# A two-block model kernel on Trainium2: feed-forward output by seven half-size products that stay in PSUM

## The chip, the cores and the metric

One core of a Trainium2 chip. The metric is the device time of one launch in microseconds (us); lower is better.

## The reference

All data is fp32, 1024 tokens of width 1024. The model is an attention-and-state-space block, then a feed-forward, then a second block of three gated branches, each with norms and residuals. The change is in the feed-forward of the first block:

```python
h = rmsnorm(x, norm_mlp_pre[l])                                   # 1024 x 1024
f = jnp.square(jax.nn.relu(h @ w_ff_in[l])) @ w_ff_out[l]         # hidden 1024 x 4096, out 1024 x 1024
x = x + rmsnorm(f, norm_mlp_post[l])
# then the second block: h = rmsnorm(x, norm_g_2); p = h @ w_in_2; ...
```

## The kernel before

**Arithmetic.** Every fp32 operand of a matmul is held as a high part (ScalarE copies it into the fp32r type) and a low part (VectorE subtracts the high part from the original). A product is three matmuls: high x high, high x low, low x high. Each takes a 128x128 stationary tile and 512 moving columns, and gives one PSUM bank. The eight banks are `A0a A0b A1a A1b X0a X0b X1a X1b`.

**Order.** There is no scheduler. Each engine runs its own program in the order in which the code is written, and semaphores tie them together. All loads go through one queue, SP's, in the order of its program; a load that waits holds up every load behind it. `FILLS` lists which product fills which bank, in TensorE's order.

**The feed-forward.** The hidden layer has 32 tiles `T` of 128 features by 1024 tokens. Four (`fi` 0 to 3) come first, then 24 from twelve panels `P` (the hidden product by seven half-size products: 7 products of 12 matmuls for a panel of two tiles), then `fi` 28 to 31. Each tile is made in one of three buffers `stage`, squared there by VectorE (`hidden_square`), and stored to HBM (`h_store`, 512 KB). VectorE's part of a panel is in `seven_run`; `seven_sums` makes the sums of weights (S1 to S4) and `seven_lo` the low parts of the weights (WL).

**The output product** (`out_part`) walks the depth of 4096 in eight chunks `c` of 512. For each chunk and each half `n` of the output columns it takes the eight token tiles `m`: 4 depth tiles x 3 matmuls into one bank. So there are 8 x 2 x 8 x 12 = 1536 matmuls. VectorE adds each bank into `F` in SBUF (`f_add`, line 1810). Chunk 0 uses the four tiles made last, which never leave SBUF; those of the other chunks are read back (`h_load`), and `W2H`/`W2L` hold two weight panels of `w_ff_out` split by `hi` (line 897) and `lo` (line 1434).

**The end of it.** For each token tile `m`: `f_square` (ScalarE, line 927), GpSimd's reciprocal root `fo` (lines 2836, 2675, 2676), `f_scale` (VectorE, lines 1886 and 1888: scale, add the residual), `x2_square` (ScalarE; it also stores the tile), GpSimd's root `x2`, `x2_norm` (VectorE, line 1892), `t2_turn` (TensorE transposes the tile, line 2214), and `t2_high`/`t2_low` split it into `XBH`/`XBL`. From these the second block's first products `au` begin. In the last chunk this chain runs tile by tile beside the remaining products.

Of the kernel before, what the change touches and what calls it, by code (L numbers as in the profile page):

```python
# [6 lines left out]
P = 128  # L7
SEQ, D = 1024, 1024
KD = D // P
# [5 lines left out]
TAU = 8  # L15
# [61 lines left out]
single("w2", 2 * FCH)  # L77
# [12 lines left out]
WHOLE = ("wo", "w2", "v2w", "w3", "plw", "P")  # L90
# [58 lines left out]
BANKS4 = ("X0a", "X0b", "X1a", "X1b")  # L149
for _c in range(FCH - 1):  # L150
    FILLS += [(("fo", _c, n, m), BANKS4[m % 4]) for n in range(2) for m in range(MT)]
for _m in range(MT):
    FILLS += [(("fo", FCH - 1, n, _m), BANKS4[(2 * _m + n) % 4]) for n in range(2)]
    if _m >= 3 and _m < 7:
        FILLS.append((("t2", _m - 3), "A%d" % ((_m - 3) % 2)))
FILLS += [(("t2", m), "A%d" % (m % 2)) for m in range(4, 8)]
# [24 lines left out]
for _m in range(MT):  # L181
    RSTD_ORDER += [("fo", _m)] + ([("x2", _m - 1)] if _m else [])
RSTD_ORDER += [("x2", MT - 1)] + [("v2", m) for m in range(MT)]
# [21 lines left out]
def hybrid_kernel(nc, io, out):  # L205
# [4 lines left out]
    with ctx:  # L210
# [83 lines left out]
        F = at("F", [P, MT, D], 34.5)  # L294
        W2H, W2L = at("W2H", [P, 2, KW, W4], 66.5, f32r), at("W2L", [P, 2, KW, W4], 82.5, f32r)
        H = at("H", [P, 5, 2, SEQ], 164.5, f32r)
        HS = at("HS", [P, 5, 2, SEQ], 164.5)
        HB, HBS = at("HB", [P, 8, 2, SEQ], 100.5, f32r), at("HBS", [P, 8, 2, SEQ], 100.5)
        post2, pre3 = at("post2", [P, D], 180.5), at("pre3", [P, D], 184.5)
        xr2 = [at("xr2_%d" % m, [P, D], (116.5 + 4 * m if m < 4 else 148.5 if m == 4 else 34.5 + 4 * (m - 5)))  # L300
# [64 lines left out]
        h_scr = dram("h_scr", [FF, SEQ])  # L365
# [35 lines left out]
        hs_ready, hidden_hi, hidden_lo = sem("hidden_squared"), sem("hidden_hi"), sem("hidden_lo")  # L401
# [65 lines left out]
        def stage_of(p, h):  # L467

            return 4 + 2 * p + h

        def hidden_of(raw_form, u):

            c, i = u // 4, u % 4
            if c in (0, 2, 4, 7):
                return (HS if raw_form else H)[:, (3, 4, 1, 0)[i]]
            return (HBS if raw_form else HB)[:, i + (4 if c == 6 else 0)]


        h_in = u_in

        def hidden_in(eng, c):
            eng.wait_ge(h_in[c % 2], 16 + 64 * ((c + 1) // 2))
# [9 lines left out]
        def _(sp):  # L492
# [10 lines left out]
            def panel(key, src):  # L503
                s = panel_free(key)
                dst = rawk[:, s] if key[0] == "w2" else raw[:, s, 0:DEPTH_K.get(key[0], KD), :]
                sp.dma_start(dst, src).then_inc(w_in_s[s], 16)
# [161 lines left out]
            wf2 = io["w_ff_out"].rearrange("o (k p) n -> p (o k) n", p=P)  # L668
# [4 lines left out]
            def w2_panel(c, n):  # L673
                g = (c - 1) % FCH
                panel(("w2", 2 * c + n), wf2[:, KW * g:KW * (g + 1), W4 * n:W4 * (n + 1)])
# [14 lines left out]

            def h_store(T):
                sp.wait_ge(hs_ready, T + 1)
                sp.dma_start(h_scr[T * P:(T + 1) * P, :], stage[T % 3][:]).then_inc(x1_out[T % 3], 16)

            def h_load(c):
                if c in (2, 3, 4, 5, 7):
                    filled(sp, ("fo", c - 3 if c == 7 else c - 2, 1, MT - 1))
                for u in range(4 * c, 4 * c + 4):
                    T = u - 4
                    staged(sp, T % 3, T // 3 + 1)  # L700
                    sp.dma_start(hidden_of(True, u)[:, 1, :], h_scr[T * P:(T + 1) * P, :]).then_inc(h_in[c % 2], 16)
            for p in RUNS[0][0]:
                seven_panel(p, wf1, 2 * P * (p + 2))
                h_store(2 * p)
                h_store(2 * p + 1)
            fi_panel(LAST_HIDDEN)
# [18 lines left out]
            for m in range(5):  # L725
                x1_in(m)
# [2164 lines left out]
```

## Time and profile before

| | |
|---|---|
| median of 3 runs | 2157.14 us (2157.02 to 2157.6) |
| the profiled execution | 2156.99 us, of which the span in the trace is 2155.3 us |
| granted TensorE clock, mean | 0.996 of full |
| TensorE busy | 2110.9 us, 9828 matmuls |
| VectorE, ScalarE, GpSimd busy | 1151.8, 749.1, 266.0 us |
| HBM traffic | 178.71 MB read, 62.39 MB written, 112 GB/s over the span |

The times of single matmuls in the trace overlap (they are pipelined and their ends are modelled), so a stage of TensorE is measured from start to start. Times of a row are counted from the start of the span.

### The profile page before, as it was taken

To read this page: it belongs to the slowest core of one execution; us is meant where nothing else is said; L and a number is where in the kernel's file an instruction comes from. 1 tells how busy PE (TensorE), PEld (TensorE's weight loads), DVE (VectorE), ACT (ScalarE), POOL (GpSimd) and SP (SyncE) were. 2 spreads that over 40 slices of the span, in tenths; PEclk is the share of its full clock that TensorE was granted. 3 is DMA by queue.
4 is the path that set the end of the run, shared out by engine and by line. 5 is a ranking of instruction groups with operands and counts; after the bars stand their busy time and mean duration, and the time that the engine had idled before them with its cause. 6 is when DMAs were issued, how large, how long until landed. Compare 5 with 4: busy or idle time off the path is not lost.

```text
span 2155.3 us, 24566 instructions
## 1 busy us (share of the span) xinstructions
PE 2110.9 (98%) x9828; PEld 1746.7 (81%) x9828; DVE 1151.8 (53%) x1326; ACT 749.1 (35%) x1112; POOL 266.0 (12%) x507
## 2 busy tenths in 40 slices
PE   7999999989999999999999999999999999999998
PEld 6888888877888888878888878888888888878877
DVE  4226666837458566423444467666444666535552
ACT  4236666143324444333111234224444333222121
POOL 1376295000110000000000021200000000000100
PEclk9999999999999999999999999999999999999999
DMA  5543323676312333322234153113323221424332
GB/s 152 120 99 103 118 93 101 168 241 231 131 69 88 108 118 118 118 98 79 78 119 155 40 185 113 40 49 108 118 106 110 79 78 64 147 97 147 117 118 108
DMA packets 169989, 243.88 MB, mean 113 GB/s; under 512 B 26995, under 2 KB 128020, under 8 KB 169620
## 3 DMA queue, kind: packets, MB, share of 16 engines
q1 hardware_dynamic: 160400, 219.64, 30.7%
q10 hardware_dynamic: 9476, 22.67, 3.3%
q8 instruction: 78, 1.28, 0.2%
q14 instruction: 35, 0.29, 0.0%
HBM read 178.71 MB, written 62.39 MB: 112 GB/s over the span
## 4 chain that ended last, share of the span: by engine, by line
PE 83%; DVE 7%; issue 4%; ACT 2%; DMA 1%; SPq 1%; POOL 1%; DVEq 0%; POOLq 0%; ACTq 0%
PE A L2160 7%; PE A L2162 7%; PE A L2161 7%; PE X L2422 6%; PE X L2423 6%; PE X L2424 6%; PE X L2497 5%; PE X L2496 5%; PE X L2498 5%; PE A L2497 4%; PE A L2496 4%; PE A L2498 4%; PE X L2160 2%; PE A L2422 2%; PE A L2423 2%
## 5 line engine op out<-in xcount | busy, mean ns | idle before, releaser
L1427 DVE TENSOR_TENSOR WL<-raw,WH 128x1024 fp32r<-128x1024 f32 (+1 forms) x110 | 115.2, 1048 | 270.9 <-ACT WH L891 270.8
L891 ACT ACTIVATE WH<-raw 128x1024 fp32r<-128x1024 f32 (+1 forms) x110 | 97.3, 885 | 302.8 <-PE A L2162 159.6
L2160 PE MATMUL A<-XH,WH 128*128 128x512 f32 x384 | 151.9, 396 | 0.0
L2162 PE MATMUL A<-XH,WL 128*128 128x512 f32 x384 | 149.8, 390 | 0.0
L2161 PE MATMUL A<-XL,WH 128*128 128x512 f32 x384 | 149.7, 390 | 0.0
L1441 DVE TENSOR_TENSOR WL<-S,WH 128x512 fp32r<-128x512 f32 x128 | 88.1, 689 | 104.3 <-ACT WH L916 103.2
L1810 DVE TENSOR_TENSOR F<-F,X 128x512 f32<-128x512 f32 x112 | 75.5, 685 | 126.9 <-PE X L2424 126.8
L1441 DVE TENSOR_TENSOR WL<-raw,WH 128x512 fp32r<-128x512 f32 x96 | 66.1, 688 | 108.4 <-ACT WH L916 108.3
L916 ACT ACTIVATE WH<-S 128x512 fp32r<-128x512 f32 x128 | 80.4, 628 | 116.9 <-PE X L2498 62.1
L2496 PE MATMUL X<-TH,WH 128*128 128x512 f32 x280 | 109.1, 390 | 0.0
L2498 PE MATMUL X<-TH,WL 128*128 128x512 f32 x280 | 109.1, 389 | 0.0
L2497 PE MATMUL X<-TL,WH 128*128 128x512 f32 x280 | 109.0, 389 | 0.0
L2422 PE MATMUL X<-W2H,H 128*128 128x512 f32 x256 | 101.1, 395 | 5.1 <-DVE H L1857 2.7
L897 ACT ACTIVATE W2H<-rawk 128x2048 fp32r<-128x2048 f32 x16 | 30.6, 1914 | 214.9 <-PE X L2424 214.9
L2423 PE MATMUL X<-W2L,H 128*128 128x512 f32 x256 | 100.3, 392 | 0.0
L2424 PE MATMUL X<-W2H,H 128*128 128x512 f32 x256 | 100.3, 392 | 0.0
L2423 PE MATMUL X<-W2L,HB 128*128 128x512 f32 x256 | 99.7, 390 | 0.0
L2424 PE MATMUL X<-W2H,HB 128*128 128x512 f32 x256 | 99.7, 390 | 0.0
L2422 PE MATMUL X<-W2H,HB 128*128 128x512 f32 x256 | 99.7, 389 | 0.0
L2496 PE MATMUL A<-TH,WH 128*128 128x512 f32 x232 | 90.4, 390 | 1.0 <-DVE WL L1441 1.0
L2160 PE MATMUL A<-XBH,WH 128*128 128x512 f32 x232 | 90.8, 391 | 0.0
L2162 PE MATMUL A<-XBH,WL 128*128 128x512 f32 x232 | 90.4, 390 | 0.0
(550 smaller groups left out, 5399.1 us busy)
## 6 DMA issues: line engine op xcount, KB each, us to landing
raw<-in_w_in SPq DMA_DIRECT2D x49, 1024.0 KB, 5.5
raw<-in_w_ff_in SPq DMA_DIRECT2D x16, 1024.0 KB, 5.4
rawk<-in_w_ff_out SPq DMA_DIRECT2D x16, 1024.0 KB, 9.3
h_scr<-stage SPq DMA_DIRECT2D x28, 512.0 KB, 2.6
g_scr<-stage SPq DMA_DIRECT2D x24, 512.0 KB, 3.6
g_scr<-gst ACTq DMA_DIRECT2D x32, 256.0 KB, 2.8
x_scr<-xr ACTq DMA_DIRECT2D x16, 512.0 KB, 2.8
HBS<-h_scr SPq DMA_DIRECT2D x16, 512.0 KB, 6.1
```

Source lines behind the costliest of these rows:

```text
L891: A(unit_home(WH[:, r % 2, 0:kb, :], key), unit_of(raw[:, SLOT[p], 0:kb, :], key, i), ACT.Copy).then_inc(w_hi, 1)
L1427: TT(unit_home(WL[:, r, 0:kb, :], key), unit_of(raw[:, SLOT[p], 0:kb, :], key, i), unit_home(WH[:, r, 0:kb, :], key).bitcast(f32), ALU.sub ...
L1441: TT(seven_home(WL, p, j), seven_weights(p, j), seven_home(WH, p, j).bitcast(f32), ALU.subtract).then_inc(w_lo, 1)
L2160: mm(dst, WH[:, r, k, :], xh, start=(k == 0), stop=False)
L2161: mm(dst, WH[:, r, k, :], xl, start=False, stop=False)
L2162: return mm(dst, WL[:, r, k, :], xh, start=False, stop=(k == kb - 1))
L2422: mm(dst, xh, wh(k), start=(k == 0), stop=False)
L2423: mm(dst, xh, wl(k), start=False, stop=False)
L2424: last = mm(dst, xl, wh(k), start=False, stop=(k == kb - 1))
L2496: mm(psum(key), high[:, i, :], xh, start=opens and i == 0, stop=False, skip_group_check=not opens)
L2497: mm(psum(key), high[:, i, :], xl, start=False, stop=False, skip_group_check=not opens)
L2498: last = mm(psum(key), low[:, i, :], xh, start=False, stop=i == KW - 1, skip_group_check=not opens)
```

## The change

The output product is now made from seven half-size products. Tokens, output columns and the depth are each cut in two: tokens into 0 to 511 and 512 to 1023, output columns into 0 to 511 and 512 to 1023, and the depth into its even and its odd tiles of 128 (a "pair" q is the tiles 2q and 2q+1). Each of the seven products j has 512 tokens x 2048 of depth x 512 columns: four token tiles, four chunks c of four depth tiles, three matmuls each. `STEPS` lists their 28 steps (j, c), each of 48 matmuls, in the order: products 0 and 1 by turns over their four chunks, then 2 and 3 by turns, then 4, 5, 6. Each product keeps its four banks over its whole depth; products 2 and 4 go on accumulating on product 1's banks, 3 and 5 on product 0's (`OUT_OPENS` names those that start from nothing). So a bank is read once in four steps, by `product_copies` (ScalarE), `join` or `last_join` (VectorE), and `f_add` is gone.

- **Hidden side.** While the hidden tiles are made, VectorE makes four sums and differences of halves of each pair (`hidden_sum`, 4 x 128x512 for each of 16 pairs) in `SB`. SP stores 256 KB of the even tile, 512 KB of the odd one, and 1 MB of sums of each pair to `a_scr`, seven half-width forms in all, in place of 512 KB a tile. The last four tiles go through memory too. A `stage` buffer is reused only when its sums are made (`summed_past`).
- **Weight side.** Products 1 to 4 need a sum of quarters of `w_ff_out`, which VectorE makes in place from what was loaded (`weights_sum`, 128x2048, one a step). Those of product 3 are stored to `w_scr` and read again for product 4.
- **Loads.** 64 loads of 1 MB for the steps go through a ring of eight 8 KB buffers (four from product 5 on; the first four loads have homes of their own). Each waits until the last user of its buffer is split. A pair of steps of products 0 and 1 takes 4 loads, of 2 and 3 takes 5 and a store, a step of 4 takes 3, of 5 and 6 takes 2.
- **Splits.** Each step splits its weights and its hidden data into `W2H`/`W2L` and `H2H`/`H2L` (two buffers each), one step ahead: `split_high` waits until the step before last is done.
- **Norms.** The chain of tiles 0 to 3 now runs beside steps 20 to 25 (r = s - 21 in the code of VectorE), the one of tiles 4 to 7 after `last_join`. Their residual rows lie in the buffers of the weight panels, so panels `au` 2 and `v2w` 0 are loaded when these tiles have been stored.

```diff
+STEPS = [(j, c) for js in ((0, 1), (2, 3), (4,), (5,), (6,)) for c in range(CHUNKS) for j in js]
...
-            for c in range(FCH - 1):
-                for n in range(2):
-                    for m in range(MT):
-                        out_part(c, n, m)
...
+            for s in range(STEP[6, 2]):
+                r = s - STEP[5, 0]
+                if r in (2, 3, 4, 5):
+                    out_step(s, range(2))
+                    t2_turn(r - 2)
+                    out_step(s, range(2, 4))
+                else:
+                    out_step(s)
+            out_step(STEP[6, 2], range(3))
+            out_step(STEP[6, 3], range(1))
+            out_step(STEP[6, 2], range(3, 4))
+            out_step(STEP[6, 3], range(1, 4))
+            t2_turn(4)
+            first_half(("au", 0), xb, "t2", 0)
             t2_turn(5)
...
+            def out_step(s, ms=range(4)):
+                j, c = STEPS[s]
+                if ms[0] == 0:
+                    pe.wait_ge(out_lo, 2 * s + 2)
+                opens = j in OUT_OPENS
+                for m in ms:
+                    key = ("S", j, m)
+                    if c == 0:
...
+                        begin(key)
+                    for k in range(KW):
+                        high, low = H2H[:, s % 2, k, P * m:P * (m + 1)], H2L[:, s % 2, k, P * m:P * (m + 1)]
+                        mm(psum(key), high, W2H[:, s % 2, k, :], start=opens and c == 0 and k == 0, stop=False, ...)
+                        mm(psum(key), high, W2L[:, s % 2, k, :], start=False, stop=False, ...)
+                        last = mm(psum(key), low, W2H[:, s % 2, k, :], start=False, ...)
...
+            def split_high(s):                                   # ScalarE
+                if s >= 2:
+                    step_past(act, s - 2)
...
+                A(W2H[:, s % 2], out_weights(s), ACT.Copy).then_inc(out_hi, 1)
+                landed(act, (j, c, "hidden"))
+                A(H2H[:, s % 2], out_hidden(s), ACT.Copy).then_inc(out_hi, 1)
...
+            def split_low(s):                                    # VectorE
+                dve.wait_ge(out_hi, 2 * s + 1)
+                TT(W2L[:, s % 2], out_weights(s), W2H[:, s % 2].bitcast(f32), ALU.subtract).then_inc(out_lo, 1)
+                dve.wait_ge(out_hi, 2 * s + 2)
+                TT(H2L[:, s % 2], out_hidden(s), H2H[:, s % 2].bitcast(f32), ALU.subtract).then_inc(out_lo, 1)
...
+            for s in range(2, len(STEPS)):                       # VectorE
+                r = s - STEP[5, 0] - 1
+                if 1 <= r < 5:
+                    x2_norm(r - 1)
+                split_low(s)
+                if s + 1 < len(STEPS) and STEPS[s + 1][0] in SUMMED:
+                    weights_sum(s + 1)
...
+                if r == 3:
+                    join(5, 0, part(4, 1), part(4, 1))
+                    join(5, 1, part(5, 1), part(5, 1))
+                if 0 <= r < 4:
+                    f_scale(r)
...
-                if m:
+                if m % 4:                                        # GpSimd: order of the roots
                     x2_rstd(m - 1)
-            x2_rstd(7)
+                if m % 4 == 3:
+                    x2_rstd(m)
```

**First place: VectorE at the start of the twelve panels.** TL are low parts of token sums, S and WL as above, `stage` rows are squares. Before:

```order
L1820 TENSOR_TENSOR TL1_195<-TR1_191,TH1_187 128x2048 [waits t_hi,t_sum]
L1455 TENSOR_TENSOR S1_202<-raw_49 128x512 [waits w_loaded1]
L1455 TENSOR_TENSOR S2_203<-S1_202,raw_49 128x512 [waits s_sum]
L1441 TENSOR_TENSOR WL_52<-raw_49,WH_51 128x512 [waits w_hi]
L1441 TENSOR_TENSOR WL_52<-S1_202,WH_51 128x512 [waits w_hi]
L1820 TENSOR_TENSOR TL2_196<-TR2_192,TH2_188 128x2048 [waits t_hi]
L1769 TENSOR_TENSOR stage2_211<-stage2_211 128x1024 [waits evicted_A0]
L1455 TENSOR_TENSOR S3_204<-raw_49 128x512
L1455 TENSOR_TENSOR S4_205<-raw_49,S2_203 128x512 [waits s_sum]
L1820 TENSOR_TENSOR TL3_197<-TR3_193,TH3_189 128x2048 [waits t_hi]
L1441 TENSOR_TENSOR WL_52<-S2_203,WH_51 128x512 [waits w_hi]
```

The same place of the change:

```order
L1992 TENSOR_TENSOR TL1_205<-TR1_201,TH1_197 128x2048 [waits t_hi,t_sum]
L1943 TENSOR_TENSOR SB0_171<-stage0_219 128x512 [waits hidden_squared]
L1943 TENSOR_TENSOR SB0_171<-stage0_219,stage1_220 128x512 [waits hidden_squared]
L1612 TENSOR_TENSOR S1_212<-raw_49 128x512 [waits w_loaded1]
L1612 TENSOR_TENSOR S2_213<-S1_212,raw_49 128x512 [waits s_sum]
...
L1992 TENSOR_TENSOR TL2_206<-TR2_202,TH2_198 128x2048 [waits t_hi]
L1943 TENSOR_TENSOR SB0_171<-SB0_171,stage0_219 128x512 [waits hidden_sum]
L1943 TENSOR_TENSOR SB0_171<-stage1_220,SB0_171 128x512 [waits hidden_sum]
L1927 TENSOR_TENSOR stage2_221<-stage2_221 128x1024 [waits evicted_A0]
...
L1992 TENSOR_TENSOR TL3_207<-TR3_203,TH3_199 128x2048 [waits t_hi]
L1598 TENSOR_TENSOR WL_52<-S2_213,WH_51 128x512 [waits w_hi]
```

Four sums of 128x512 stand ahead of the WL of the panel's third product, where there were none.

**Second place: VectorE while the first token tiles are normed.** Before, beside the last chunk (F<-F,X adds a bank, F<-F is `f_scale`, F<-xr2 is `x2_norm`):

```order
L1886 SCALAR_TENSOR_TENSOR F_156<-F_156,vec_53,post2_163 128x1024 [waits rstd_made]
L1888 TENSOR_TENSOR xr2_2_167<-xr2_2_167,F_156 128x1024 [waits x2_loaded,dve_chain]
L1810 TENSOR_TENSOR F_156<-F_156,X1 128x512 [waits evicted_X1b,tile_done]
L1892 SCALAR_TENSOR_TENSOR F_156<-xr2_1_166,vec_53,pre3_164 128x1024 [waits rstd_made]
L1810 TENSOR_TENSOR F_156<-F_156,X0 128x512 [waits evicted_X0a,tile_done]
```

In the change, in steps 22 to 24 (W2L and H2L are the low parts of the next step):

```order
L2060 SCALAR_TENSOR_TENSOR F_156<-F_156,vec_53,post2_173 128x1024 [waits rstd_made]
L2062 TENSOR_TENSOR xr2_1_176<-xr2_1_176,F_156 128x1024 [waits x1_loaded,dve_chain]
L2066 SCALAR_TENSOR_TENSOR F_156<-xr2_1_176,vec_53,pre3_174 128x1024 [waits rstd_made]
L2033 TENSOR_TENSOR W2L_158<-ring3_166,W2H_157 128x2048 [waits out_split_hi]
L2035 TENSOR_TENSOR H2L_160<-ring2_165,H2H_159 128x2048 [waits out_split_hi]
L2060 SCALAR_TENSOR_TENSOR F_156<-F_156,vec_53,post2_173 128x1024 [waits rstd_made]
L2062 TENSOR_TENSOR xr2_2_177<-xr2_2_177,F_156 128x1024 [waits x2_loaded,dve_chain]
L1631 TENSOR_TENSOR XBL_142<-A0,XBH_141 128x8x128 [waits xt_hi]
L2066 SCALAR_TENSOR_TENSOR F_156<-xr2_2_177,vec_53,pre3_174 128x1024 [waits rstd_made]
L2033 TENSOR_TENSOR W2L_158<-ring1_164,W2H_157 128x2048 [waits out_split_hi]
L2035 TENSOR_TENSOR H2L_160<-ring0_163,H2H_159 128x2048 [waits out_split_hi]
L2056 TENSOR_TENSOR F_156<-X0,F_156 128x512 [waits tile_done] x2
```

The tile's `x2_norm`, which waits for GpSimd, now stands ahead of both low parts that TensorE's next step waits for.

## Rows read from the trace of the kernel before

**Rows 1.** Page, part 1: busy us (share of the span), number.

```profile
PE 2110.9 (98%) x9828; PEld 1746.7 (81%) x9828; DVE 1151.8 (53%) x1326; ACT 749.1 (35%) x1112; POOL 266.0 (12%) x507
```

**Rows 2.** Page, part 4: chain that ended last, by engine.

```profile
PE 83%; DVE 7%; issue 4%; ACT 2%; DMA 1%; SPq 1%; POOL 1%; DVEq 0%; POOLq 0%; ACTq 0%
```

**Rows 3.** Windows: stretch, length, busy us and number by engine, clock, DMA share, GB/s.

```profile
760.00:779.00 19.00, 19.00 (x86) 15.74 (x85) 11.37 (x17) 7.93 (x14) 0.00 (x0) 1.00 0.31 111
...
997.00:1001.00 4.00, 4.00 (x19) 3.34 (x18) 2.54 (x3) 0.00 (x0) 0.00 (x0) 1.00 0.97 354
```

**Rows 4.** Timeline of TensorE where the output product begins: start, duration, work.

```profile
942.61 0.39 PE L2160 MATMUL A<-XBH,WH 128*128 128x512 f32 x1
...
945.33 0.39 PE L2422 MATMUL X<-W2H,H 128*128 128x512 f32 x1
...
947.14 0.39 PE L2424 MATMUL X<-W2H,H 128*128 128x512 f32 x1
950.22 0.79 PE L2422 MATMUL X<-W2H,H 128*128 128x512 f32 x1 [2.69 <-DVE H L1857]
...
953.37 0.42 PE L2423 MATMUL X<-W2L,H 128*128 128x512 f32 x1
```

**Rows 5.** Instructions on tile W2H: number, duration ns min/median/max.

```profile
L2422 PE MATMUL X<-W2H,H x256: 387/390/794, 945.3 to 1305.2; 128*128 128x512 f32 x128
...
L897 ACT ACTIVATE W2H<-rawk x16: 1901/1917/1918, 928.0 to 1254.6; 128x2048 fp32r<-128x2048 f32 x16
L1434 DVE TENSOR_TENSOR W2L<-rawk,W2H x16: 2291/2293/2293, 929.9 to 1256.6; 128x2048 fp32r<-128x2048 f32 x16
```

**Rows 6.** Timeline of VectorE at the start of the panels.

```profile
677.82 0.68 DVE L1441 TENSOR_TENSOR WL<-S,WH 128x512 fp32r<-128x512 f32 x1
678.42 0.68 DVE L1441 TENSOR_TENSOR WL<-raw,WH 128x512 fp32r<-128x512 f32 x1
```

**Rows 7.** Timeline of TensorE there.

```profile
677.23 0.39 PE L2498 MATMUL X<-TH,WL 128*128 128x512 f32 x1
678.65 0.47 PE L2496 MATMUL A<-TH,WH 128*128 128x512 f32 x1 [1.04 <-DVE WL L1441]
```

**Rows 8.** Timeline of TensorE at the last chunk's first tile.

```profile
1256.26 0.39 PE L2424 MATMUL X<-W2H,H 128*128 128x512 f32 x1
1259.03 0.47 PE L2422 MATMUL X<-W2H,H 128*128 128x512 f32 x1 [2.39 <-DVE W2L L1434]
```

**Rows 9.** Timeline of all engines at the end of the output product.

```profile
1307.92 0.63 ACT L927 ACTIVATE junk_c<-F 128x512 f32<-128x512 f32 x1 [1.41 <-DVE F L1810]
...
1308.72 0.41 POOL L2836 TENSOR_TENSOR vec<-vec 128x1 f32<-128x1 f32 x1 [3.65 <-ACT junk_c L927]
...
1310.13 1.28 DVE L1886 SCALAR_TENSOR_TENSOR F<-F,vec,post 128x1024 f32<-128x1024 f32 x1
...
1311.44 1.23 DVE L1888 TENSOR_TENSOR xr<-xr,F 128x1024 f32<-128x1024 f32 x1
...
1312.26 1.91 PE L2214 MATMUL A<-ident,F 128*128 128x128 f32 x16
...
1313.07 1.06 ACT L927 ACTIVATE F<-xr 128x1024 f32<-128x1024 f32 x1 [3.39 <-DVE xr L1888]
1313.13 1.28 DVE L1892 SCALAR_TENSOR_TENSOR F<-xr,vec,pre 128x1024 f32<-128x1024 f32 x1 [0.46 <-POOL vec L2676]
...
1313.93 0.47 PE L2160 MATMUL X<-XBH,WH 128*128 128x512 f32 x1
...
1314.31 0.22 POOL L2675 TENSOR_SCALAR vec<-vec 128x1 f32<-128x1 f32 x1 [1.22 <-ACT F L927]
...
1314.62 0.57 POOL L2676 TENSOR_TENSOR vec<-vec 128x1 f32<-128x1 f32 x1
...
1317.85 1.02 ACT L935 ACTIVATE XBH<-A 128x1024 fp32r<-128x1024 f32 x1 [1.80 <-PE A L2214]
...
1322.63 1.98 PE L2168 MATMUL X<-XBH,WH 128*128 128x512 f32 x8
```

More of the change, by code:

```diff
@@ L148 @@
 FILLS += [(("fi", t), "A%d" % (t % 2)) for t in range(LAST_HIDDEN, 4 * FCH)]
[L149 to L156, printed above, removed]
+BANKS4 = {"X": ("X0a", "X0b", "X1a", "X1b"), "A": ("A0a", "A0b", "A1a", "A1b")}
@@ L157, with split_past @@
+def split_past(load):
+    j, c, what = load
+    s = STEP[j, c]
+    if what == "hidden":
+        return 2 * s + 2
+    if (j, what) in ((0, (0, 0)), (2, (1, 1))):
+        return 2 * s + 3
+    return 2 * s + 1
 TAIL = [("au", 0), ("au", 1), ("au", 2), ("ws", 0), ("au", 3)] + [("v2", m) for m in range(MT)]
@@ L1297, in _ @@
             filled(act, ("t2", 7))
-            for m in range(4, MT):
-                act.wait_ge(x2_out[m], 16)
             hi(("v2w", 0))
@@ new lines, in weights_sum @@
+            def weights_sum(s):
+                j, c = STEPS[s]
+                dst = out_weights(s)
+                for load in LOADS:
+                    if load[:2] == (j, c) and load[2] != "hidden":
+                        landed(dve, load)
+                if j == 3:
+                    dve.wait_ge(w_sum, SUM_NO[s] - 1)
+                other = {1: (0, c, (0, 0)), 2: (2, c, (0, 1)), 3: (2, c, (1, 1)), 4: (4, c, "sum")}[j]
+                if j == 1:
+                    landed(dve, other)
+                TT(dst, dst, load_home(other), ALU.add if j == 3 else ALU.subtract).then_inc(w_sum, 1)
@@ L1884, in f_scale, with part, join @@
+            def part(row, n):
+                return F[:, row, W4 * n:W4 * (n + 1)]
+            def join(j, m, dst, other):
+                filled(dve, ("S", j, m))
+                TT(dst, psum(("S", j, m)), other, ALU.add).then_inc(evicted[BUF["S", j, m]], 1)
             def f_scale(m):
@@ L1909, in _, with last_join @@
+            def last_join(m):
+                freed(dve, ("S", 0, m))
+                join(6, m, part(4 + m, 0), part(4 + m, 0))
+            last_join(0)
+            f_scale(4)
+            last_join(1)
+            last_join(2)
+            x2_norm(4)
+            f_scale(5)
+            last_join(3)
+            f_scale(6)
+            t2_low(4)
+            x2_norm(5)
             f_scale(7)
             x2_norm(6)
-            t2_low(4)
+            t2_low(5)
             x2_norm(7)
-            for m in range(5, MT):
-                t2_low(m)
+            t2_low(6)
@@ L1917, in _ @@
+            t2_low(7)
             lo(("au", 2))
```

504 lines of the change are left out of this document (312 added, 192 removed).

## Prediction

> **What bounds the kernel now.** I read the page first. TensorE is busy 98% of the span, VectorE 53%, ScalarE 35%, GpSimd 12% [rows 1], and the chain that ended last runs over TensorE for 83% [rows 2]. So the other engines and the loads count only where TensorE waits for them. A busy TensorE says nothing of its rate; that comes from starts. Twelve matmuls of the hidden product start within 945.33 - 942.61 = 2.72 us [rows 4], 0.2267 us each. In the trace's own terms a matmul lasts 0.39 us, but the next has long begun.
>
> Next, the stretch that the change rewrites. Its first matmul starts at 945.33 [rows 4]. As its end I take 1322.63, where the second half of the first `au` product starts, since both kernels have done the same there [rows 9]. That is 377.3 us. In it lie 1536 matmuls of the output product (by the code; one of its six groups has 256 [rows 5]), 48 of `au`, and 8 turns of eight transposes; two turns take 1313.93 - 1312.26 = 1.67 us [rows 9], one 0.84. Work: 1584 x 0.2267 + 8 x 0.84 = 359.1 + 6.7 = 365.8 us. The other 11.5 us are waits. The reader can see two: chunk 0 waits for its last hidden tile, from 947.37 (947.14 and one pitch) to 950.22, and then seven matmuls to 953.37 take 3.15 us in place of 1.59, since the clock is at its half level [rows 4]; and the last chunk waits for its weights, 1256.49 to 1259.03 [rows 8]. The rest are short waits for norms at the end.
>
> **The change, term by term.** All against the profiled execution's 2156.99 us, which is 0.15 below the median of the runs.
>
> *Fewer matmuls.* 7 products x 4 chunks x 48 = 1344 in place of 1536: 192 x 0.2267 = **-43.5 us**. Same shape, same columns, so the same pitch.
>
> *The waits of before go*: **-11.5**. Step 0 reads tiles made long ago: its split stands in ScalarE's and VectorE's programs ahead of the last two hidden tiles, some 10 us before TensorE needs it. What waits take their place comes next.
>
> *Splits between steps.* A step lasts 48 x 0.2267 = 10.9 us. The next one's split may begin when the step before is done: high part of the weights 1.92, low part 2.29 behind it, and the second low part another 2.29 behind that, in all 6.5 us; then a sum of weights, about one more 2.29 [rows 5]. 8.8 of 10.9: hidden, with 4.4 us to spare for the split that TensorE waits for. `join` (0.68 for 128x512 [rows 6]) comes at most four times a step, 2.7 us, and eats into that reserve, not into TensorE's time. Cost **0**; were the cover gone, each microsecond over would be paid up to 27 times.
>
> *Loads.* 64 loads and 4 stores of 1.05 MB are 71 MB in 28 x 10.9 = 305 us, 234 GB/s; at the densest, products 2 and 3, six in two steps: 6.3 MB in 21.8 us, 289 GB/s. Product 4 asks for the same. Where the old kernel loads hidden tiles and weights together, the engines are 97% busy at 354 GB/s [rows 3]. So the peak demand is 82% of what is shown, and the ring reaches about two steps ahead. Followed load by load, the closest one (product 4's second sum) may start some 13 us before VectorE wants it, behind a store and two loads, with some 5 us over. Cost **0**, and this is the term that I know least.
>
> *Norms of tiles 0 to 3 beside steps 20 to 25.* Here I expect a new wait. VectorE's order is: `f_scale(r)`, next iteration `x2_norm(r)`, then the two low parts. Between them lie ScalarE and GpSimd, and GpSimd makes the root x2 of a tile only after the root fo of the next one. The cycle, from [rows 5, 9]: `f_scale` 1310.13 to 1311.44 + 1.23, 2.54; square of x2 ends at 1314.13, 1.46; two squares of the next tile, 0.63 and 0.80 till GpSimd starts; fo 1308.72 to 1310.13, 1.41; x2 1314.31 to 1315.19, 0.88; `x2_norm` 1.28; low parts 2 x 2.29. Sum 13.6 us, and 14.6 where `t2_high` (1.02) gets between on ScalarE. TensorE's steps with a turn last 11.7. The reserve of the first ones is used up after two cycles: counted from the start of step 20, `f_scale(0)` starts at 6.5, and the split for step 24 is ready at 6.5 + 2 x 13.6 + 14.6 = 48.3; `join` of product 5's first bank 49.0. TensorE would be there at 4 x 10.9 + 2 x 0.84 = 45.2. **+3.7** at step 24 (0 if the engines hand over sooner than full durations add up; 6 with a clock drop).
>
> *The end.* From product 6's first bank full, TensorE has 48 matmuls (10.9 us) before it wants token tile 4. That tile: join 0.7, squares 1.4, fo 1.4, `f_scale` 2.5, square 1.5, then the squares of tile 5 (1.4), fo of 5 (1.4), x2 of 4 (0.9), `x2_norm` 1.3: 12.5. Wait 1.6. For tile 5 VectorE has 2.5 + 0.7 + 2.5 + 1.2 + 1.3 = 8.2 more, TensorE 0.8 + 24 x 0.2267 = 6.3: wait 1.9. Then tile 6 0.2, and 1.0 since `au` 0 now follows tile 7's turn directly and needs its `t2_high`. Together **+4.7** (1 to 8). Panel `au` 2 is now loaded only after tile 5 is stored, but its split waits for `au` 0 to leave the WH buffer anyway, some 14 us later: 0.
>
> *Hidden sums.* 64 x 0.6 to 0.7 us on VectorE. In a panel of 19.0 us VectorE is busy 11.4 [rows 3]; four more make 14.1, and the sums stand where a spare was: 0. But at the start of the panels VectorE is already what TensorE waits for: product 2's first matmul starts at 678.65 where 677.46 was possible, 0.15 after WL (677.82 + 0.68) [rows 6, 7]. Four sums ahead of that WL push it by 4 x 0.62 = **+2.5**. The gap becomes 3.7 us. A gap of 2.85 halved the clock for seven matmuls [rows 4], one of 2.54 is followed by a matmul of 0.47 us, not 0.79, so it did not [rows 4, 8]; I take the price of the former, 3.15 - 1.59 = **+1.5**.
>
> *Stores* of 1.75 MB in place of 1 MB a panel, with a panel's weights: 2.9 MB in 19 us, about 150 GB/s: 0.
>
> Sum: -43.5 - 11.5 + 3.7 + 4.7 + 2.5 + 1.5 = -42.6. 2156.99 - 42.6 = **2114 us**.
>
> **A rule weighed.** The trace has the weight loads of before, whose four 2 KB rows a partition lie 512 KB apart, at 354 GB/s together with hidden tiles [rows 3]; those of the change lie 1 MB apart. The Trainium skill (DMA: Bandwidth & Descriptors, Latency and other measured facts) says that copies whose rows per partition are a large power of two apart slow down: 207 GB/s at 512 KB, 164 at 2 MB. This trace does not agree for the spacing within a partition. By the rule the estimate would be under 207 GB/s, the loads would be the bound, and the sum would end above the time of before. It is the third rival.
>
> **The rivals.**
> 1. *The panels lose time.* If VectorE's sums hold up one WL or one eviction a panel by their own length, 12 panels x 1.2 (two sums) = 14 us: 2128. For it: they stand between evictions. Against: 4.9 us of each panel stay idle, and WL is made four products ahead. Chance 10%.
> 2. *The loads are a little late.* If the mix with stores gives 250 GB/s, two steps of products 2 and 3 take 25.2 in place of 21.8, four times, and a step of product 4 12.6 in place of 10.9, four times: 13.6 + 6.8 = 20 us, less what the ring holds: 2130. For it: reading back what was just written, and a single queue. Chance 9%.
> 3. *The loads bound the whole stretch, and the kernel is slower.* With residual rows, norms and stores of x2 the stretch moves 79 MB. At 207 GB/s that is 382 us in place of 305 + 8: 2114 + 69 = 2183. It decides from 79 MB / (305 + 51) = 222 GB/s down. For it: the spacing of the weight rows. Against: 354 GB/s with half that spacing. Chance 5%.
> 4. *No new waits at all.* -43.5 - 11.5 and nothing given back: 2102. Chance 5%, since the wait at the panels' start is nearly certain.
>
> **The numbers.** My forecast, 2107 to 2121, has 71%. The range is to reach into rivals 1 and 2: 2105 to 2130. A run tells a change of 0.2%, 4.3 us, from none. Faster 94%, same 1%, slower 5%.
>
> **What the profile of the changed kernel would show.** 9636 matmuls (9828 less 192). Pitch 0.227 in the steps, 10.9 us from step to step. No wait at step 0. A gap of about 3.7 us at the panels' third product and a half-level clock behind it. A wait of TensorE of 3 to 4 us at step 24, put down to VectorE, with `x2_norm` late behind GpSimd. Then four waits that add up to 5 before `au` 0's second half, which starts about 47 us earlier after the output product's first matmul than before. DMA at about 290 GB/s and 80% busy in products 2 to 4. It would be wrong if TensorE or ScalarE waits for DMA landings in the steps, or if `split_high` starts late behind a sum of weights, step after step.

## The result, and the profile after

| | before | changed |
|---|---|---|
| median | 2157.08 us (4 runs, 2153.43 to 2157.6) | 2125.39 us (4 runs, 2123.24 to 2128.78) |
| profiled execution, its span | 2156.99, 2155.3 us | 2126.21, 2124.5 us |
| TensorE busy, matmuls | 2110.9 us, 9828 | 2074.2 us, 9636 |
| bytes moved by all DMA queues | 243.88 MB | 298.40 MB |

The ratio is 0.9858, 95% interval 0.9841 to 0.9875: 1.4% faster, within the range, and 11 us above the forecast of 2114.

The page of the changed kernel, part 1 (busy us, share of the span, number), answers to [rows 1]:

```profile
PE 2074.2 (98%) x9636; PEld 1714.3 (81%) x9636; DVE 1217.5 (57%) x1322; ACT 789.6 (37%) x1116; POOL 261.7 (12%) x507
```

TensorE is as full as before with 192 matmuls less. So the 30.8 us between the spans are best found by four landmarks on TensorE, read from the starts of matmuls in both timelines. Behind each landmark both kernels have the same work left, except for the 192 matmuls of the output product. The first is the place in the attention output's product (wo) where TensorE waits for the low part of its weights (WOL), some 12 us after that product's first matmul:

| stretch | before | changed | difference |
|---|---|---|---|
| start to the wait inside wo | 544.85 | 543.58 | -1.3 |
| to the panels' third product | 133.80 | 136.32 | +2.5 |
| to the output product's first matmul | 266.68 | 277.07 | +10.4 |
| to `au` 0's second half | 377.30 | 331.25 | -46.05 |
| to the end | 832.67 | 836.28 | +3.6 |

The rewritten stretch gave what the sum said; the loss lies ahead of it and behind it. TensorE's timeline of the changed kernel at the places where it waited (start, duration; in brackets the idle time and what ended it), which answers to [rows 4, 7 to 9]:

```profile
676.03 0.39 PE L2727 MATMUL X<-TH,WL 128*128 128x512 f32 x1
679.90 0.77 PE L2725 MATMUL A<-TH,WH 128*128 128x512 f32 x1 [3.48 <-DVE WL L1598]
...
927.25 0.39 PE L2391 MATMUL A<-XBH,WL 128*128 128x512 f32 x1
932.42 0.77 PE L2389 MATMUL A<-XBH,WH 128*128 128x512 f32 x1 [4.79 <-DVE WL L1584]
...
938.11 0.42 PE L2390 MATMUL A<-XBL,WH 128*128 128x512 f32 x1
...
956.97 0.39 PE L2744 MATMUL X<-W2H,H2H 128*128 128x512 f32 x1
...
1219.70 0.39 PE L2747 MATMUL X<-W2H,H2L 128*128 128x512 f32 x1
1222.91 0.47 PE L2744 MATMUL X<-W2H,H2H 128*128 128x512 f32 x1 [2.82 <-DVE F L2056]
...
1270.89 0.33 PE L2443 MATMUL A<-ident,F 128*128 128x128 f32 x1 [1.84 <-DVE F L2066]
...
1278.73 0.33 PE L2443 MATMUL A<-ident,F 128*128 128x128 f32 x1 [1.28 <-DVE F L2066]
...
1288.22 0.50 PE L2397 MATMUL X<-XBH,WH 128*128 128x512 f32 x1 [1.11 <-ACT XBH L1071]
```

The gap of 5.17 us at 932.42, counted from start to start, is in no term of the sum. It stands at fi 30, a tile of the hidden layer, before the output product begins, and 13 matmuls behind it take 5.69 us in place of 13 x 0.2267 = 2.95. Windows of the changed kernel (columns as in [rows 3]) show the clock there at half, and at full behind the gap of step 24. The panel has VectorE at 13.81 of 19 us. In the four windows of the steps TensorE has no wait. Two of them are the densest stretches, steps 2 and 3 (from 978.74) and step 16 (from 1131.10):

```profile
760.00:779.00 19.00, 19.00 (x85) 15.74 (x84) 13.81 (x20) 7.89 (x15) 0.00 (x0) 1.00 0.47 153
...
932.40:938.10 5.70, 5.68 (x13) 4.45 (x14) 5.60 (x6) 0.84 (x1) 0.00 (x0) 0.50 0.53 202
...
978.74:1000.50 21.76, 21.76 (x98) 18.02 (x97) 11.19 (x5) 7.45 (x4) 0.00 (x0) 1.00 1.05 392
...
1050.00:1100.00 50.00, 50.00 (x223) 41.39 (x221) 30.12 (x14) 16.28 (x9) 0.00 (x0) 1.00 0.84 291
1100.00:1150.00 50.00, 50.00 (x222) 41.42 (x221) 37.60 (x23) 19.38 (x14) 0.00 (x0) 1.00 0.92 340
1131.10:1142.00 10.90, 10.90 (x50) 9.03 (x49) 9.01 (x7) 4.20 (x3) 0.00 (x0) 1.00 1.03 396
...
1222.90:1226.00 3.10, 3.09 (x14) 2.54 (x15) 3.06 (x4) 0.00 (x0) 0.00 (x0) 1.00 0.81 229
```

Why fi 30's low part was late stands one row above it, in the timeline of VectorE:

```profile
930.45 0.69 DVE L1943 TENSOR_TENSOR SB<-stage 128x512 f32<-128x512 f32 x1 [11.37 <-DMA a_scr<-SB]
931.06 1.22 DVE L1584 TENSOR_TENSOR WL<-raw,WH 128x1024 fp32r<-128x1024 f32 x1
```

The first sum of pair 14 reuses the buffer of pair 12's sums and waits 11.37 us for their store. The low part is not late by itself; it is queued behind that sum. And why the store was late stands in SP's queue:

```profile
912.42 0.36 SPq L803 DMA_DIRECT2D H2R<-a_scr  x1
912.83 0.65 SPq L803 DMA_DIRECT2D W2R<-in_w_ff_out  x1
913.89 0.36 SPq L803 DMA_DIRECT2D H2R<-a_scr  x1
914.30 1.12 SPq L803 DMA_DIRECT2D W2R<-in_w_ff_out  x1
915.46 2.65 SPq L780 DMA_DIRECT2D a_scr<-SB  x1
```

Four loads of 1 MB go first, which ScalarE first reads at 929.54 us, then the store. The sums had been ready since 909.3 (the last one starts at 908.64 and takes 0.68). The store was issued 6 us later and landed 14.9 us after its issue, at 930.4, behind the loads.

### The profile page after: what moved, and what is told of

It is laid out like the page before. It is cut to its first block, busy times and chain, and to the rows that moved or that the text cites. A ratio compares the mean times of both kernels' runs of the same rounds, so it can differ in the third digit from the quotient of the medians.

```text
span 2124.5 us, 24285 instructions
## 1 busy us (share of the span) xinstructions
PE 2074.2 (98%) x9636; PEld 1714.3 (81%) x9636; DVE 1217.5 (57%) x1322; ACT 789.6 (37%) x1116; POOL 261.7 (12%) x507
## 2 busy tenths in 40 slices
DMA packets 201413, 298.40 MB, mean 140 GB/s; under 512 B 27699, under 2 KB 128724, under 8 KB 200020
## 3 DMA queue, kind: packets, MB, share of 16 engines
q8 instruction: 77, 1.26, 0.2%
## 4 chain that ended last, share of the span: by engine, by line
PE 81%; DVE 8%; issue 5%; ACT 2%; DMA 2%; SPq 1%; POOL 1%; ACTq 0%; DVEq 0%; POOLq 0%
PE A L2389 7%; PE A L2391 6%; PE A L2390 6%; PE X L2725 5%; PE X L2727 5%; PE X L2726 5%; PE A L2725 4%; PE A L2727 4%; PE A L2726 4%; PE X L2389 2%; PE A L2651 2%; PE A L2652 2%; PE A L2653 2%; PE X L2391 2%; PE X L2390 2%
## 5 line engine op out<-in xcount | busy, mean ns | idle before, releaser
L2033 DVE TENSOR_TENSOR W2L<-ring,W2H 128x2048 fp32r<-128x2048 f32 x26 | 59.6, 2291 | 89.1 <-ACT W2H L1377 89.1
L2744 PE MATMUL X<-W2H,H2H 128*128 128x512 f32 x256 | 100.2, 391 | 3.0 <-DVE F L2056 2.8
L2747 PE MATMUL X<-W2H,H2L 128*128 128x512 f32 x256 | 99.7, 389 | 0.0
L2746 PE MATMUL X<-W2L,H2H 128*128 128x512 f32 x256 | 99.6, 389 | 0.0
L1377 ACT ACTIVATE W2H<-ring 128x2048 fp32r<-128x2048 f32 x26 | 49.8, 1914 | 123.3 <-PE A L2747 72.9
L2390 PE MATMUL A<-XBL,WH 128*128 128x512 f32 x232 | 91.3, 393 | 0.0
L2726 PE MATMUL A<-TL,WH 128*128 128x512 f32 x232 | 91.2, 393 | 0.0
L2727 PE MATMUL A<-TH,WL 128*128 128x512 f32 x232 | 91.2, 393 | 0.0
```

Of the source, the lines that this page charges most:

```text
L2390: mm(dst, WH[:, r, k, :], xl, start=False, stop=False)
L2726: mm(psum(key), high[:, i, :], xl, start=False, stop=False, skip_group_check=not opens)
L2727: last = mm(psum(key), low[:, i, :], xh, start=False, stop=i == KW - 1, skip_group_check=not opens)
L2744: mm(psum(key), high, W2H[:, s % 2, k, :], start=opens and c == 0 and k == 0, stop=False, skip_group_check=not opens)
L2746: mm(psum(key), high, W2L[:, s % 2, k, :], start=False, stop=False, skip_group_check=not opens)
L2747: last = mm(psum(key), low, W2H[:, s % 2, k, :], start=False, stop=c == CHUNKS - 1 and k == KW - 1, skip_group_check=not opens)
```

## The experiments

Each was timed beside the kernel before, on one chip; between groups of experiments the chip differed, and the median of the kernel before lay between 2156.36 and 2157.17 us. Edits are to the changed kernel unless said. The changed kernel was run again as well:

> The changed kernel once more, not edited, to see what of its differences to the first experiments is chance. Theory: the gaps that follow from the order of the programs come again to 0.1 or 0.2 us (3.87 at the panels' third product, 3.21 at step 24, 2.23 and 1.67 at the turns), the one at fi 30 to 0.5 us (5.17 to 5.59 so far, since it hangs on a store's landing), and the median is 2124 to 2127. Rival: the median moves by 4 us or more between calls, and the experiments whose effect is 2 to 3 us say nothing by their times.

2125.63 us (0.9857, 0.984 to 0.9873). The gaps came again: 3.90, 5.31, 3.21, 2.22, 1.66. What did not come again is the clock behind them: at the panels' third product 7 matmuls ran at the half level here and 13 in the first profile, and behind the unchanged gap of step 24 eight did here and none there. So 1 or 2 us between medians say nothing by themselves, but the same gaps in the traces do.

**The store ahead of the loads.**

```diff
+            sum_store(12)
             h_store(LAST_HIDDEN - 2)
             h_store(LAST_HIDDEN - 1)
             filled(sp, ("P", 11, 6))
             out_loads((0, 0), (1, 0))
-            sum_store(12)
             sum_store(13)
```

> The only edit: the store of the sums of pair 12 stands in SP's program ahead of the two stores of tiles 26 and 27, and so ahead of the first four 1 MB loads of the output product, not behind them. Theory: in the changed kernel TensorE waited 5.17 us (927.25 to 932.42, in place of one pitch of 0.23) and ran 13 matmuls at half rate behind it (2.7 us more), because a buffer of sums came free late: VectorE's first sum of pair 14 waited 11.37 us for that store, and fi 30's low part stood behind the sum. With the store ahead of the loads it should land by about 916 us, and fi 30's low part should be made when fi 30's high part is. The gap goes, and the clock stays: 4.9 + 2.7 = 7.6 us, median about 2118 and at least 5 us under the changed kernel's 2125.4. Rival: the store is slow by itself (1 MB while four loads share the engines), so that an early issue only trades places with the loads, and the first steps then wait for their loads: then a gap of 2 us or more stays here or comes at step 0, and under 3 us is won.

2117.94 us (2116.47 to 2119.28), 7.5 us under the changed kernel. The store is now issued at 910.68 us and landed 4.3 us later. In its timeline TensorE runs through, and VectorE's sum waits for nothing:

```profile
910.68 0.36 SPq L780 DMA_DIRECT2D a_scr<-SB  x1
...
920.45 0.69 DVE L1943 TENSOR_TENSOR SB<-stage 128x512 f32<-128x512 f32 x1
921.06 1.22 DVE L1584 TENSOR_TENSOR WL<-raw,WH 128x1024 fp32r<-128x1024 f32 x1
```

No gap over 0.5 us is left from 900 us to the output product, and none came at step 0. From the panels' third product to the output product it takes 269.41 us in place of 277.07, so the 7.7 us stand where they were expected. The order on the queue was the cause.

**The sums behind the low parts.**

```diff
-            hidden_sum(0, 0)
-            hidden_sum(0, 1)
...
-            hidden_sum(0, 2)
-            hidden_sum(0, 3)
             hidden_square(2)
...
             seven_lo(0, 2)
             seven_lo(0, 3)
+            for n in range(4):
+                hidden_sum(0, n)
```

> The only edit: at the start of the panels, the four hidden sums of pair 0 stand behind the low parts of the third and fourth products' weights on VectorE, not ahead of them. Theory: TensorE's gap at the panel's third product (3.87 us from start to start, with 3.48 of it put down to VectorE's WL) is the 1.4 us of before plus the four sums (2.5 us); and the 13 matmuls at half rate come from that idle stretch. Expected: gap back to about 1.4 us, no half-rate matmuls, 2.5 + 2.7 = 5.2 us less, median about 2120. Rival: the buffer of tile 3 is now held longer (ScalarE's copy of fi 3 waits for the third sum), so the wait moves to the fifth product, whose high and low parts stand behind that copy on ScalarE: then a new gap of 1 us or more some 5 to 8 us later, and under 3 us is won.

2126.5 us: nothing won. The gap became 5.48 us, and ended on another engine:

```profile
675.17 0.39 PE L2725 MATMUL X<-TH,WL 128*128 128x512 f32 x1
680.65 0.79 PE L2723 MATMUL A<-TH,WH 128*128 128x512 f32 x1 [5.09 <-ACT c L1297]
```

ScalarE's timeline of the same run shows what held it:

```profile
670.85 0.62 ACT L1052 ACTIVATE WH<-raw 128x512 fp32r<-128x512 f32 x1
679.09 1.02 ACT L1349 ACTIVATE stage<-A 128x1024 f32<-128x1024 f32 x1 [7.62 <-DVE SB L1943]
680.01 0.59 ACT L1297 ACTIVATE c<-A 128x512 f32<-128x512 f32 x1
```

The low parts were ready at 677.04 (676.36 + 0.68). But ScalarE's copy of tile 3 waits for the third sum, and the eviction `c<-A`, which frees the bank of the third product, stands behind that copy. The rival had the right mechanism one product too late. So the first three sums stay where they are; the best version below moves only the fourth, for which nobody waits there.

**`x2_norm` behind the low parts.**

```diff
-                if 1 <= r < 5:
-                    x2_norm(r - 1)
                 split_low(s)
+                if 1 <= r < 5:
+                    x2_norm(r - 1)
```

> The only edit: in steps 22 to 25 VectorE makes x2_norm of the token tile behind the two low parts of the next step, not ahead of them. Theory of the prediction: the wait of 3.21 us at step 24 comes from a cycle ScalarE - GpSimd - VectorE in which x2_norm waits for GpSimd's root and the low parts wait behind it. Expected: the gap at step 24 and the 0.61 us one behind it go, the two t2 turns in the steps are still on time, some 3 us less: median about 2122. Rival: x2_norm, made 4.6 us later, is then late for the transposes in the middle of a step, or pushes the joins of product 5 and so the end of the chain: the wait shows up at the turns or before au 0, and the sum of the gaps from step 20 to au 0's second half stays within 1 us.

2122.98 us; from first matmul to `au` 0's second half 329.65 in place of 331.25. The gap at step 24 fell from 3.21 to 2.10 only, and the one behind it (0.61) went:

```profile
1222.29 0.47 PE L2744 MATMUL X<-W2H,H2H 128*128 128x512 f32 x1 [1.70 <-DVE F L2056]
```

L2056 is `join`. So of the 3.0 us over a pitch, 1.1 hung on the order of norm and low parts. The 1.9 that are left are for the bank: product 6 takes the banks of product 5, whose joins stand behind `x2_norm` either way.

**The root of tile 4 ahead of fo 5.** In GpSimd's order `fo 4, fo 5, x2 4` became `fo 4, x2 4, fo 5`.

> The only edit: GpSimd makes the root x2 of token tile 4 directly behind fo 4, ahead of fo 5. Theory: at the end of the output product TensorE waits 2.0 us at the turn of tile 4 and 1.4 us at that of tile 5 because x2_norm(4) waits for a root that stands behind fo 5 and so behind two squares of tile 5 (about 2.5 us of chain). Expected: the wait at tile 4's turn goes (2 us), that at tile 5's turn stays or grows by up to 1 us, since VectorE's f_scale(5) stands behind x2_norm(4): 1 to 2 us less in all, median about 2124, less than the timing can tell; the trace decides. Rival: the chain is bound by VectorE's own work (4.1 us of scale, add and norm for each tile), not by GpSimd's order: then au 0's second half starts at the same time after step 24.

2125.17 us, which says nothing; the stretch took 329.89 us, 1.4 less. Tile 4's turn no longer waits, tile 5's waits 1.96 where it was 1.28. So the rival, by which `au` 0's second half starts no earlier, does not hold.

**All four together.** The second edit in the form that the second experiment allows:

```diff
             hidden_sum(0, 2)
-            hidden_sum(0, 3)
-            hidden_square(2)
...
             seven_lo(0, 3)
+            hidden_sum(0, 3)
+            hidden_square(2)
```

and in step 24 `x2_norm(2)` behind `join(5, 1)`.

> Four edits together: the early store of pair 12's sums (as in the first experiment); at the panels' start only the fourth hidden sum of pair 0 and the square of tile 2 stand behind the third and fourth low parts (the first three sums stay ahead, since ScalarE's copy of tile 3, and the evictions behind it, wait for the third); x2_norm behind both low parts in steps 22 to 25, and in step 24 behind product 5's first two joins too; root x2 of tile 4 ahead of fo 5. Theory: each edit takes its own wait: the gap at fi 30 and its slow matmuls 7.6, the gap at the panels' third product from 3.87 to 3.87 - 0.6 - 1.15 = 2.1 us with no half-rate matmuls behind it (1.8 + 2.7), step 24 from 3.2 to under 0.6 (2.7), tile 4's turn 1.5 net: 2125.4 - 16.3 = 2109 us, which is within 5 us of what was forecast for the change itself. Rival: the start of the panels is bound by ScalarE and not by VectorE's order (as the second experiment's 5.48 us gap, ended by an eviction, allows), so the gap stays over 3 us and the median is about 2113.

2109.85 us (0.9777, 0.9763 to 0.9792), 15.5 us under the changed kernel and 47 under the one before, as expected (2109); the gap at the panels' third product is 2.04 us, so the rival is refuted. The profiled execution was the fastest of its runs, at 2107.58. Its timeline of TensorE:

```profile
677.62 0.47 PE L2726 MATMUL A<-TH,WH 128*128 128x512 f32 x1 [1.65 <-DVE WL L1598]
...
1207.87 0.47 PE L2745 MATMUL X<-W2H,H2H 128*128 128x512 f32 x1 [0.51 <-DVE F L2056]
```

From the third product to the output product it takes 944.26 - 677.62 = 266.64 us, before 266.68: the hidden sums in the panels cost nothing in it. At step 24 some 0.7 us are left, at step 25 1.1.

**More traffic.** Behind each load of a step, a copy from HBM to HBM that nobody reads, of 256 KB and of 512 KB:

```diff
                 sp.dma_start(load_home(load), src).then_inc(slot_in[i][0], 16)
+                sp.dma_start(d_scr[LOADS.index(load)]..., wf2[0][:, 4 * c:4 * c + 2, 0:W4]).then_inc(d_in, 16)
```

> The changed kernel, and behind each of the 64 loads of the steps a copy of 256 KB of weights from HBM to HBM on the same queue, whose result nobody reads: traffic that the kernel doesn't need. Theory: the loads have room. In steps 8 to 19 they and four stores move 37.8 MB in 130.6 us; with the copies, counted once, 46.2 MB, 354 GB/s, just what the trace of before showed at 97% busy: 0 to 4 us more. Rival: a single queue with waits for buffers in it is already near its limit, and a quarter more costs a quarter of a step in each of the 12 steps: 33 us.

> As the one before, with 512 KB copied behind each load. Theory: steps 8 to 19 now ask for 54.6 MB, which at 360 GB/s takes 152 us in place of 130.6: 21 us more, all of it in steps 8 to 19 as TensorE's waits for ScalarE's or VectorE's splits that wait for landings; steps 0 to 7 and 20 to 27 stay at 10.9 us. Rival: HBM to HBM copies pass twice, so that already half of this traffic bounds the stretch: 60 us and more.

With 256 KB 2127.82 us: the stretch stays at 331.3 us, and the gap at fi 30 grows from 5.17 to 7.16, since more traffic goes ahead of the store. With 512 KB 2136.34 us: the stretch takes 338.75, the gap at fi 30 is 9.85. Windows of the latter:

```profile
1050.00:1100.00 50.00, 50.00 (x222) 41.41 (x221) 31.09 (x14) 19.09 (x11) 0.00 (x0) 1.00 1.01 379
1100.00:1150.00 50.00, 46.98 (x201) 38.41 (x200) 29.44 (x17) 17.15 (x12) 0.00 (x0) 0.97 1.03 397
```

The bound shows itself at about 400 GB/s (379 to 402 in these stretches, with the engines busy all the time), not at 354 or 360; so my 21 us were 7.5. There is one wait for a landing: at 1140.24 TensorE starts 3.41 us after its last matmul, since VectorE waited 4.39 us for a load to make a sum of weights. These copies are also a second witness for the cause at fi 30: nothing else was changed there than what the queue carries.

**Sums made twice** into a spare buffer, pairs 1 to 12:

> The changed kernel, with each hidden sum of pairs 1 to 12 made a second time into a spare buffer that nobody reads: four more VectorE instructions of 0.6 to 0.7 us in each of the twelve panels. Theory: in a panel of 19.04 us VectorE is busy 13.8, and its waits are for evictions that come at TensorE's pace; with 16.5 it still has 2.5 us over, so the panel keeps 19.04 us, +0 to 3 us in all. Rival: the sums stand between evictions and weights' low parts, and the order holds TensorE up well before VectorE is full: 1 us a panel or more, 12 us in all.

2127.7 us. From the panels' third product to the output product it takes 277.34 us (277.07 without), and fi 30's gap alone is 0.5 longer. VectorE is busy 15.77 of 19 us, TensorE still all 19:

```profile
762.00:781.00 19.00, 19.00 (x86) 15.72 (x85) 15.77 (x24) 7.89 (x15) 0.00 (x0) 1.00 0.47 153
```

**The last 3.6 us.** Behind the output product nothing was edited, yet the last product (W3H) starts behind a gap of 3.22 us, before of 1.70. TensorE's timeline, before and changed:

```profile
2060.98 0.47 PE L2422 MATMUL X<-W3H,NH 128*128 128x512 f32 x1 [1.31 <-issue]
...
2027.62 0.76 PE L2651 MATMUL X<-W3H,NH 128*128 128x512 f32 x1 [2.83 <-issue]
```

> The kernel before once more, for a second profile of it. In the one at hand TensorE waits 1.70 us from start to start where the last product (W3H) begins, at full clock; in all profiles of the changed kernel and its variants it is 3.1 to 4.0 us, mostly with half-rate matmuls behind it, though no instruction there was changed. Theory: the landing of that load varies from run to run, and here the gap is anything from 1.7 to 4: then the 3.6 us that the changed kernel loses behind the output product are no cost of the change. Rival: it is 1.7 us again, and the difference is the program's (the place of a load in memory or in time), whose cause stays open.

1.73 us again, in a profiled execution of 2152.0 us. Every kernel made from the changed one so far has 3.1 to 4.0, so it was not chance. The transfers of the changed kernel, from 2016 to 2023.5 us in 40 equal slices (GB/s), and its queues:

```profile
GB/s 0 0 0 0 0 0 0 0 169 158 169 197 300 306 355 328 257 306 295 377 382 371 388 371 311 186 175 77 38 27 22 22 38 235 235 147 109 279 377 350
...
q1 hardware_dynamic: 1347, 1.36, 59.2%
q8 instruction: 1, 0.02, 1.8%
```

The load that ScalarE waits for has a tail of about 1 us at 22 to 38 GB/s, a sixteenth to a tenth of the rate that all 16 transfer engines reached, and there is one packet of the queue "instruction", which starts 1.1 us after the load's issue. In both profiles of before that packet comes some 12 us after the load's issue, when it has long landed. Two experiments move it, by waits that are fulfilled already and stand at the start of TensorE's program, where it idles until 8.63 us:

```diff
             pe.wait_ge(id_in, 16)
+            for _ in range(80):
+                pe.wait_ge(id_in, 16)
```

> The four edits of the fifth experiment, and 80 waits at the start of TensorE's program that are already fulfilled, in time that TensorE idles anyway. In all profiles of the changed kernel one packet of the queue named instruction (0.02 MB) falls into the load of W3's second half, whose traffic then ends with some 1.3 us at 22 to 27 GB/s; in both of the kernel before it falls elsewhere, and W3's product starts 1.7 us earlier. The page counts 77 such packets, one each 32 us. Theory: they are TensorE's program being fetched, one transfer engine is held up by each, and the last of 16 shares of the load lands late. The waits shift the fetch some 5 us ahead of the load (from 2002.5 to about 1997.7): the gap at W3 falls from 3.44 to about 1.7 us, median 2108. Rival: the packet belongs to another engine's program or has nothing to do with the tail: then it stays where it is, or moves and the gap stays at 3.1 us or more.

> The mirror of the one above: the kernel before, with 132 fulfilled waits at the start of TensorE's program, which should shift its fetch from 2063.0 to about 2053.7, into the load that W3's second half waits for (issued at 2051.4, landed by 2056). Theory: the gap at W3 grows from 1.70 to over 3 us, with half-rate matmuls behind it in some runs: 1.5 to 4 us more, 2158 to 2161. Rival: it stays at 1.7 us wherever the packet falls.

With 80 waits in the best version the packet lies at 2000.5 to 2001, ahead of the load (issued at 2002.60), and the gap fell from 3.44 to 1.64 us:

```profile
2012.12 0.47 PE L2654 MATMUL X<-W3H,NH 128*128 128x512 f32 x1 [1.25 <-issue]
```

The median is 2108.52 us, 1.3 lower, which is within what two runs of a kernel differ. In the traces, `au` 0's second half to the end takes 832.09 us in place of 833.37. With 132 waits in the kernel before, the packet fell into the load, the same tail of 23 GB/s came (view as above, from 2051 to 2058), and the gap grew from 1.70 to 3.13 us:

```profile
GB/s 0 0 0 0 53 176 129 252 345 363 363 369 456 357 374 363 351 357 363 357 374 328 111 23 23 23 23 23 29 23 94 228 211 187 275 374 339 345 380 398
...
q8 instruction: 1, 0.02, 1.0%
```

and in TensorE's timeline:

```profile
2061.72 0.47 PE L2424 MATMUL X<-W3H,NH 128*128 128x512 f32 x1 [2.74 <-issue]
```

2159.64 us against 2156.89, ratio 1.0016 (1.0007 to 1.0025): the unchanged kernel made slower by 132 waits that wait for nothing. An obvious rival is that the waits cost time where they stand. They do move TensorE's first matmul from 8.58 to 12.46 us, but at the wait inside wo 0.26 us of that is left (545.11 against 544.85), and the last matmul ahead of W3 starts 0.7 us earlier than before (2058.59 against 2059.28). The span is 2.3 us longer all the same, so the loss lies behind it. The theory holds both ways: where the packet falls decides the gap. That one transfer engine's share of the load comes last because of it fits the tail at a sixteenth of the rate, but no view here shows a single engine.

## Why the prediction was right, and where it was off

**Fewer matmuls, waits of before, splits.** -43.5 - 11.5 with the splits at 0 was right to the microsecond: with the waits that I did expect (3.7 and 4.7) the rewritten stretch should take 377.3 - 46.6 = 330.7 us, and took 331.25.

**Step 24 and the end.** Step 24 cost 3.21 - 0.23 = 3.0 and the next one 0.4 (forecast 3.7); the turns of tiles 4 and 5 2.0 and 1.4, and `au` 0's second half 1.1 (forecast 4.7 in all). At step 24 it was product 5's first joins that came last, as in the prediction's chain (49.0 against 48.3 for the split). 1.1 us of the wait hung on the norm ahead of the low parts, 1.2 more on the norm ahead of the joins (the gap is 3.21, then 2.10, then 0.89 in the fifth experiment). The fourth rival, no new waits, is refuted.

**Loads.** At 0, right: no wait of TensorE for a landing in 28 steps. The demand of 289 GB/s was well sized as a mean (291 in the window from 1050, 340 in the one from 1100), but the queue moves it in bursts: steps 2 and 3 moved 392 GB/s, step 16 moved 396. So my limit of 354 GB/s was too low. The second and third rivals are refuted, and the sixth and seventh experiments say by how much: in the seventh the stretch moves 112 MB in place of 81 and takes 7.5 us more; 402 GB/s were moved from 1000 to 1050 us of it. The Trainium skill (DMA: Bandwidth & Descriptors, Latency and other measured facts) gives its 207 GB/s at a row pitch of 512 KB for copies between HBM tensors, with one row of 16 KB for each partition, so that the pitch lies between partitions. The third rival took that over to another pattern: in half of the loads here the rows of neighbouring partitions lie 4 KB apart, and only the four rows of one partition 1 MB. These loads are not slowed to that rate (392 GB/s in steps 2 and 3); no run here has the pattern that the Trainium skill names.

**Hidden sums.** In the panels 0, right, even when made twice; the first rival is refuted. At the panels' start +2.5 was right (2.52), but the low clock behind it cost 5.68 - 13 x 0.2267 = 2.7, where I took 1.5 from a shorter gap. How long the clock stays low there is not fixed by the gap: in the second run of the changed kernel the same gap (3.90 us) was followed by 7 slow matmuls in 3.12 us, which is just my 1.5.

**Stores. The step that failed.** "*Stores* of 1.75 MB in place of 1 MB a panel, with a panel's weights: 2.9 MB in 19 us, about 150 GB/s: 0." That is an argument on bandwidth, and on bandwidth it is right. What it leaves out is that a store gives back one of two buffers of sums, and that on a queue in program order it stood behind 4 MB of loads. It cost 5.17 - 0.23 = 4.9 us and 2.7 of low clock: 7.6 of the missing 11.8, shown by the first experiment, which won 7.7 us in that stretch of its trace and 7.5 in the median.

**Behind the stretch**, which I had at nothing: +3.6. Of this, 1.5 is the longer gap, where a packet of TensorE's program meets a load that is waited for, shown both ways. The half-rate matmuls behind it cost 2.9 (14 in 6.11 us; the granted clock is 0.67 from 2027.6 to 2037 us, before 1.00). The other 0.8 us came back elsewhere, which is not explained. In the eleventh experiment, with the packet ahead of the load, this stretch takes 832.09 us, before 832.67. The change edits nothing here; that its shorter program moved the packet is the likely reason, and not tested by itself. The remaining -1.3 ahead of the wo product is a load's landing, which in other runs of the same code came early or late by 4 us (a gap at 458 us of 4.56 us in the first profile of before and of 0.66 in the second, where ScalarE waits for a tile read back from HBM).

Sum of what was off: 7.6 + 1.2 + 0.5 + 3.6 - 1.3 = 11.6, of 11.8 (42.6 forecast, 30.8 measured between the two spans). So 2125.39 us lies above the 2107 to 2121 to which I gave 71%. It lies within 2105 to 2130 only since the range reached into rivals 1 and 2, and both are refuted: the store at fi 30, the largest miss, is in none of the four. That the range held is luck.

## What to carry to other kernels

When a change adds stores, ask of each not only its bytes but which buffer it gives back, what stands ahead of it in its queue, and what stands behind the instruction that waits for the buffer. Let stores that free buffers go ahead of loads that are only early. Before a piece of work is moved behind a critical one, follow all three engines: here a sum on VectorE held a copy on ScalarE, and behind that the eviction that TensorE needed.

## What the hardware showed beyond that

- TensorE's program is fetched in packets: the page of the changed kernel counts 77 with 1.26 MB on that queue, 16 KB each. One that met the 1 MB load let it land after 6.7 us, where 5.0 to 5.2 is usual; over all profiles in which that load met one it is 6.5 to 7.5. It matters only if that load is waited for: in the kernel before a packet at 2063.37 us meets the next such load (issued at 2060.91, landed after 6.62 us), and TensorE has no gap for it.
- The clock behind a gap is no fixed function of the gap. 2.82 us idle at step 24 left it at full in the changed kernel (window above) and halved it for several matmuls in the first experiment and in the second run of the changed kernel, with the same gap. The window of the first experiment:

```profile
1216.50:1220.00 3.50, 3.49 (x9) 2.82 (x10) 3.46 (x5) 0.18 (x1) 0.00 (x0) 0.57 0.83 242
```

- In the traces here the clock fell behind every idle stretch of 3.1 us or more. Below that both occur, down to 1.92 us: behind the wait of 1.9 to 2.0 us near 484 us, which is in all 14 traces, the next matmuls ran at the half level in six of them and at full in eight. The longest stretch without a fall was 3.05 us (the fifth experiment, at 2011.85). The window behind the wait of 1.92 us in the second experiment:

```profile
483.40:488.00 4.60, 4.54 (x13) 3.58 (x14) 2.79 (x3) 1.07 (x2) 0.00 (x0) 0.63 0.62 179
```

- What decides there stays open. A fall cost from 1.3 us (6 matmuls in 2.69, at W3 in the first experiment) to 2.9 (14 in 6.11, there in the changed kernel) where it happened; at step 24 of the first experiment only 0.9 of it reached the end of the stretch (332.14 in place of 331.25).
